# Layer norm of a 256 x 1024 activation: the root's Newton steps on GpSimd, the mean taken off on VectorE meanwhile

## The reference

```
def layer_norm(x, g, b):
    xf = x.astype(jnp.float32)
    mu = jnp.mean(xf, -1, keepdims=True)
    var = jnp.mean(jnp.square(xf - mu), -1, keepdims=True)
    y = (xf - mu) * lax.rsqrt(var + LN_EPS)
    return (y * g.astype(jnp.float32) + b.astype(jnp.float32)).astype(x.dtype)
...
x = layer_norm(alpha * x + mix, ln_g[l, 1], ln_b[l, 1])
```

## Time and profile before

| what | us |
|---|---|
| median of 3 runs (1609.17 to 1610.27) | 1610.07 |
| the profiled execution, whole | 1608.99 |
| its span in the profile | 1607.2 |
| PE busy | 1572.9 (98%) |
| DVE busy | 997.8 (62%) |
| ACT busy | 704.6 (44%) |
| POOL busy | 18.5 (1%) |

### The profile page before, as it was taken

One profiled execution on the slowest core, in us unless ns is written; L12 is line 12 of the kernel. 1 busy time (PEld: TensorE's weight loads), 2 busy tenths in 40 slices (PEclk: granted clock), 3 DMA queues, 4 the chain that ended last, 5 costly groups with the idle time before them and its releaser, 6 DMA issues.

```text
span 1607.2 us, 23932 instructions
## 1 busy us (share of the span) xinstructions
PE 1572.9 (98%) x10298; PEld 1425.8 (89%) x10298; DVE 997.8 (62%) x1282; ACT 704.6 (44%) x794; POOL 18.5 (1%) x77
## 2 busy tenths in 40 slices
PE   6999999999999999999999999999999999999997
PEld 6879998799899988999988899998999898789996
DVE  6776556768765567535677654466354768964546
ACT  4725344457354443334354343344343365343431
POOL 1000000000000000000000000000000000000000
PEclk9999999999999999999999999999999999999999
DMA  8346555543565556555463655546555563375551
GB/s 264 130 157 210 184 185 182 209 158 111 172 207 193 184 184 199 193 185 184 145 223 132 210 184 184 186 155 236 184 184 184 157 208 97 126 236 184 186 189 46
DMA packets 198456, 286.18 MB, mean 178 GB/s; under 512 B 9287, under 2 KB 167055, under 8 KB 198351
## 3 DMA queue, kind: packets, MB, share of 16 engines
q1 hardware_dynamic: 194943, 272.20, 51.5%
q0 software_dynamic: 3264, 11.93, 2.3%
q10 hardware_dynamic: 144, 0.52, 0.1%
HBM read 283.58 MB, written 1.05 MB: 177 GB/s over the span
## 4 chain that ended last, share of the span: by engine, by line
PE 84%; DVE 11%; ACT 3%; DMA 1%; issue 1%; SPq 0%; DVEq 0%; ACTq 0%
PE ps L395 79%; DVE wlo L293 2%; PE ps L428 2%; ACT whi L288 1%; DVE x L508 1%; DVE res L505 1%; DVE xt L467 1%; DVE stats L482 1%; DMA raw<-in_mla_w_dq 1%; DVE res L479 1%; DMA raw<-in_w_in_mlstm 1%; DVE nt L497 1%; PE ps L1509 1%; PE ps L1821 0%; PE ps L1314 0%
## 5 line engine op out<-in xcount | busy, mean ns | idle before, releaser
L395 PE MATMUL ps<-xt,whi 128*128 128x256 f32 x4016 | 727.8, 283 | 0.0
L293 DVE TENSOR_TENSOR wlo<-raw,whi 128x2048 fp32r<-128x2048 f32 (+2 forms) x259 | 576.0, 2254 | 116.0 <-ACT whi L288 115.5
L395 PEld LDWEIGHTS ps<-xt,whi 128*128 128x128 f32 x4016 | 629.7, 192 | 8.0 <-issue 3.6
L395 PE MATMUL ps<-xt,wlo 128*128 128x256 f32 x2008 | 568.2, 283 | 0.0
L288 ACT ACTIVATE whi<-raw 128x2048 fp32r<-128x2048 f32 (+2 forms) x262 | 483.5, 1879 | 20.2 <-DMA raw<-in_w_out 4.5
L395 PE MATMUL ps<-whi,yt 128*128 128x512 f32 (+1 forms) x1472 | 461.4, 386 | 1.7 <-DVE wlo L293 0.9
L395 PEld LDWEIGHTS ps<-xt,wlo 128*128 128x128 f32 x2008 | 385.2, 192 | 0.0
L395 PEld LDWEIGHTS ps<-whi,yt 128*128 128x128 f32 x1472 | 274.8, 188 | 56.9 <-DVE wlo L293 2.2
L395 PE MATMUL ps<-wlo,yt 128*128 128x512 f32 (+1 forms) x736 | 283.8, 386 | 0.0
L709 DVE SCALAR_TENSOR_TENSOR arena<-arena,ps 128x512 f32<-128x512 f32 x76 | 52.2, 686 | 368.9 <-issue 289.9
L395 PE MATMUL ps<-whi,xt 128*128 128x512 f32 (+4 forms) x778 | 220.0, 361 | 3.8 <-DVE wlo L293 2.8
(11 more groups left out here) (220 smaller groups left out, 710.9 us busy)
## 6 DMA issues: line engine op xcount, KB each, us to landing
raw<-in_ffn_w_up SPq DMA_DIRECT2D x76, 1024.0 KB, 5.3
raw<-in_ffn_w_down SPq DMA_DIRECT2D x76, 1024.0 KB, 4.9
raw<-in_ffn_w_gate SPq DMA_DIRECT2D x44, 1024.0 KB, 5.3
raw<-in_diff_w_qkv SPq DMA_DIRECT2D x12, 1024.0 KB, 5.2
raw<-in_w_in_conv SPq DMA_DIRECT2D x10, 1024.0 KB, 6.0
raw<-in_w_out SPq DMA_DIRECT2D x8, 1024.0 KB, 4.9
raw<-in_w_in_mlstm SPq DMA_DIRECT2D x7, 1024.0 KB, 7.5
raw<-in_w_in_mlstm SPq DMA_DIRECT2D x8, 768.0 KB, 4.2
```

Source lines behind the costliest of these rows:

```text
L293: nc.vector.tensor_tensor(wlo[:, u.slot, 0:u.size], raw[:, u.slot, 0:u.size], whi[:, u.slot, 0:u.size].bitcast(F32), ALU.subtract).then_in ...
L395: m = nc.tensor.matmul(out_, p, q, start=first and n == 0, stop=last and n == 2, skip_group_check=True)
```

## The change

After the seed, the six Newton instructions of each row block are issued by GpSimd instead of VectorE, as tensor_scalar with y (and w) as per-partition scalars, each waiting for the one before it. A new semaphore ln_seed tells GpSimd that v, w and the seed are there, and ln_root tells VectorE that the root is. VectorE issues both halves' (res - mean) * g right after the seed, without waits between them, then waits for ln_root and issues both halves' second instruction. v is now waited for before w is issued, and the seed is issued after w without a wait of its own. GpSimd's loop now runs over ten norms instead of nine, and the load of the next g and b follows its Newton steps.

```
-            link.mark(nc.vector.tensor_scalar_add(v, mv[:, t, 1:2], LN_EPS))
+            link(nc.vector.tensor_scalar_add(v, mv[:, t, 1:2], LN_EPS))
             link.mark(nc.vector.tensor_scalar(w, mv[:, t, 1:2], LN_EPS, -0.5, ALU.add, ALU.mult))
-            dve.wait_ge(link.s, link.n - 1)
-            link(nc.vector.tensor_scalar(y.bitcast(I32), v.bitcast(I32), -0.5, RSQRT_SEED,
-                                         ALU.mult, ALU.add))
-            for _ in range(3):
-                link(nc.vector.scalar_tensor_tensor(out=k, in0=y, scalar=w, in1=y, op0=ALU.mult,
-                                                    op1=ALU.mult))
-                link(nc.vector.scalar_tensor_tensor(out=y, in0=k, scalar=1.5, in1=y,
-                                                    op0=ALU.add, op1=ALU.mult))
+            nc.vector.tensor_scalar(y.bitcast(I32), v.bitcast(I32), -0.5, RSQRT_SEED,
+                                    ALU.mult, ALU.add).then_inc(ln_seed, 1)
             if t == 0:
                 dve.wait_ge(gb_loaded, 32 * (n + 1))
             for h in range(2):
                 half = slice(h * 512, h * 512 + 512)
-                link(nc.vector.scalar_tensor_tensor(
+                link.mark(nc.vector.scalar_tensor_tensor(
                     out=res[:, t, half], in0=res[:, t, half], scalar=mv[:, t, 0:1],
                     in1=gb[:, 0, half], op0=ALU.subtract, op1=ALU.mult))
+            dve.wait_ge(ln_root, 2 * n + t + 1)
+            for h in range(2):
+                half = slice(h * 512, h * 512 + 512)
+                dve.wait_ge(link.s, link.n - 1 + h)
                 nc.vector.scalar_tensor_tensor(
                     out=x[:, t, half], in0=res[:, t, half], scalar=y, in1=gb[:, 1, half],
                     op0=ALU.mult, op1=ALU.add).then_inc(ln_x, 1)
...
+        def ln_gpsimd(pool, step, n):
+
+            for t in range(TT):
+                w, k, y = nt[:, 1, TT + t:TT + t + 1], nt[:, 0, t:t + 1], rs[:, t:t + 1]
+                pool.wait_ge(ln_seed, 2 * n + t + 1)
+                for i in range(3):
+                    step(nc.gpsimd.tensor_scalar(k, y, w, y, ALU.mult, ALU.mult))
+                    if i < 2:
+                        step(nc.gpsimd.tensor_scalar(y, k, 1.5, y, ALU.add, ALU.mult))
+                    else:
+                        nc.gpsimd.tensor_scalar(y, k, 1.5, y, ALU.add, ALU.mult).then_inc(ln_root, 1)
+            if n < N_LN - 1:
+                pool.wait_ge(ln_x, 4 * (n + 1))
+                load_gb(pool, n + 1)
...
-            for n in range(N_LN - 1):
-                ln_gpsimd(pool, n)
+            step = Chain(pool, pool_step)
+            for n in range(N_LN):
+                ln_gpsimd(pool, step, n)
```

More of the change, by code:

```diff
@@ L345, in build @@
         acc_bank = sem("acc_bank")
+        ln_seed = sem("ln_seed")
+        ln_root = sem("ln_root")
+        pool_step = sem("pool_step")
         ln_x = sem("ln_x")
@@ L510, in ln_normal @@
                     op0=ALU.mult, op1=ALU.add).then_inc(ln_x, 1)
-        def ln_gpsimd(pool, n):
-            pool.wait_ge(ln_x, 4 * (n + 1))
-            load_gb(pool, n + 1)
+        def ln_gpsimd(pool, step, n):
[11 more added lines that the diff above has]
+                load_gb(pool, n + 1)
         def load_gb(pool, n):
```

## The result

The changed kernel takes 1628.49 us (median of 4 runs, 1625.97 to 1629.15), the kernel before 1610.17 beside it: a ratio of 1.0113, interval 1.01 to 1.0126. It is 18.3 us slower. The profiled execution is the shortest of the four, 1625.97 with a span of 1624.1, 16.9 longer than before's 1607.2.

A forecast was written before the change was run, and what follows sets the result against it. PE was taken to bound the kernel, busy 98% of the span, with VectorE counting only where PE waits. Delays of 10.35+0.37+0.74+0.44 = 11.9 us on the median 1610.07 gave 1622.0; range 1611 to 1637.

The forecast's parts named there:

- held back: Rival: GpSimd's first Newton instruction waits for VectorE's two subtractions, R 1.07 later, +26.9 us, 1637; chance 0.30.
- the prediction's own signs: Prediction wrong if the step is not near 0.52, the first instruction waits, or PE's restart follows half 1.
- PE waits for half 0: At row block 1, PE's restart comes 2.88 us after half 0's second instruction starts; half 1's catching up buys nothing.
- The hand-over to GpSimd: From the seed's end on VectorE to GpSimd's first Newton instruction: 0.31 us, taken from a GpSimd load.
- Six steps of 0.28 and five waits of 0.24: GpSimd's Newton chain in each row block: 2.88 us, against 1.34 on VectorE.
- Unheld: Main case: GpSimd's Newton steps run beside VectorE's subtractions without waiting, steps of 0.4 to 0.6, 1622 us; chance 0.50.
- The sum per norm: Row block 1 of norms 0 to 8: PE's restart 1.15 us later each, 10.35 together.
- R: Start of half 0's second instruction on VectorE: forecast S+3.47 instead of S+2.32, or S+4.54 if held.
- S: Start of the seed instruction in the kernel before, 109.83 in norm 0, row block 1; other times count from it.
- Row blocks 0: Delay where VectorE has no slack: 0.37 us each in norms 4 and 6, 0.22 each in 7 and 8.
- The delay given back: Rival: a late weight transfer, as after norm 7, swallows no more than 1 to 2 us; no separate chance given.
- Norm 9: No PE work follows; its last half, which opens the last output transfer, comes 0.37 us later.

The follow-up runs named there:

- Three kernels that keep their clock there: Against the changed kernel: subtraction input from PSUM, 1610.82 us; two Newton steps, 1614.34. Against the kernel before: both subtractions ahead of both second instructions, 1612.59.
- the second trace of the changed kernel: The changed kernel run again unaltered, as a control for later runs: 1627.09 us, ratio 1.0108 against the kernel before.
- root first: Against the changed kernel, VectorE waits for the root before it issues both halves' subtractions: 1633.94 us, ratio 1.0152 against the kernel before.
- VectorE's order: Against the kernel before, Newton stays on VectorE and both subtractions go ahead of both second instructions: 1612.59 us, ratio 1.0021.

## Why the prediction came out as it did

The forecast was 1622.0, slower; measured 1628.5, within the range and with the right sign. Its mechanism was not the one that acted: the rival "held back" was, at a smaller size than the 1637 forecast for it. By the prediction's own signs it failed: a step is 0.40 from start to start (111.74 to 112.55 is 0.81 for two), not 0.52, and the first instruction waits.

- **PE waits for half 0, and its restart follows at 2.88** behind half 0's second instruction. Right: in the changed kernel 113.65 to 116.53 is 2.88. The reordering on VectorE alone showed that half 1's catching up buys nothing.
- **The hand-over to GpSimd, 0.31.** It was 0.10. The load that I took it from is another kind of instruction. Back again it was 0.04 (113.35+0.26 to 113.65), forecast 0.06.
- **Six steps of 0.28 and five waits of 0.24, 2.88.** The instructions take 0.34 and 0.26, near the upper bound I had chosen (mean 0.30). The wait is not 0.24 but 0.10. Together 2.3 without a hold. This term was mis-sized by 0.6: one wait of GpSimd, between a memset and a select, does not price the wait between two steps.
- **Unheld.** This is the step that failed. GpSimd's first instruction was held by the two subtractions: it ran from 110.28 to 111.64, 1.36 instead of 0.34. With an input from PSUM it was not held, with one subtraction for 0.43. I had 1.07 for it in the rival; it is 1.02. The rule of the Trainium skill that I cited ("SBUF — State Buffer", "Who interferes with whom") is what this case then showed, and I had given it 0.30.
- **The sum per norm.** R was put at S+3.47 without the hold and S+4.54 with it. S is agg+0.43 in the kernel before (109.83-109.40). Counted from agg, so that it doesn't matter that this whole norm lies 0.14 later in the second trace, R is agg+4.11, that is S+3.68. The error of 0.8 in hand-over and waits and the missing hold of 1.02 nearly cancel, which is why 1.15 a norm was forecast and 1.34 to 1.40 came. A near hit in the sum was two misses in its terms.
- **Row blocks 0.** I counted norms 4, 6, 7 and 8, 1.2 in all. Norms 1 and 3 cost 0.34 each as well, and all six come to 2.5. Norms 1 and 3 have the same 0.15 of idle time behind row block 0 as norms 7 and 8, and I had called them free without looking at it.
- **The clock.** Not in the sum at all. A wait of PE of 2.3 to 2.4 was followed by some microseconds at 1.2 GHz after norm 7 in both traces of the changed kernel and after norm 1 in one of them; the growth there was 1.2 to 1.4 above that of the other norms (2.70 and 2.55 after norm 7, 2.75 after norm 1, others 1.34 to 1.42). After norm 7 the low clock took more than this difference shows, since 0.9 is given back there: an estimate is 2.70-1.37+0.9 = 2.2 for the 6.8 us at half clock, beside 1.4 for the 3.4 us after norm 1.
- **The delay given back.** I allowed 1 to 2 us for it, behind norm 7, and named a weight transfer as the place. Three kernels that keep their clock there give back 0.9; 0.72 of it is PE's wait for VectorE's small instruction (line 2103), not a transfer. In the changed kernel that wait is gone too, and the low clock covers it.
- **What is missing from the sum.** The first trace lies 16.9 above before's, 5.0 more than the 11.9 forecast: nine restarts 0.22 too small (2.0), row blocks 0 (1.3), the clock less what norm 7 gives back (1.3), the end (0.25), 4.85 together, and 0.15 that lay before the first norm. The median lies 1.4 further off than the profiled execution; no trace shows that part, though the second trace of the changed kernel, of an execution of 1627.30, has 1.4 more than the first behind norm 1, by the clock.
- **Norm 9.** Forecast 0.37 for its end, measured 0.62; the same error of R makes 0.21 of the difference.

Left open: the last 0.2 of what is given back behind norm 7; why the clock fell after a PE wait of 2.44 in one execution and not after 2.43 in another; and where it fell in the executions that were not profiled.

## What to carry to other kernels

Before work is moved to GpSimd to run beside VectorE, look at VectorE's inputs: an instruction with two SBUF inputs stopped a GpSimd instruction that reads SBUF until it was done here, and the overlap that was the point of the move was worth little: of the 1.34 that the two subtractions take, 1.02 came back as GpSimd's hold. With one input in PSUM the overlap was whole, and the kernel was as fast as before, not faster. Even then a chain of six dependent 128x1 instructions took GpSimd 2.3 us against VectorE's 1.34. To hide something in the gaps of such a chain, put independent instructions of the same engine into them, first the ones on which the first consumer waits.

## What the runs showed of the hardware that was not expected

- GpSimd's wait between two dependent small instructions is 0.10 us and its start behind VectorE's semaphore 0.10; its 128x1 tensor_scalar takes 0.34 with two per-partition scalars and 0.26 with one. The 0.24 that stood before a select is not general.
- The hold ends 0.14 to 0.22 after the end of VectorE's last instruction with two SBUF inputs, and the second of two that are issued back to back comes ahead of a GpSimd instruction that has already begun to wait: GpSimd was not let in between.
- Waits of PE that differ by 0.01 us (2.43, 2.44) were followed by the full clock in one execution and by half of it in another; waits of 1.02 and 0.80 close together were followed by half clock for 3.4 us, and in one execution (root first) a wait of 2.75 kept the full clock and one of 1.91 did not.
- A wait of PE can hide elsewhere: behind norm 7 with VectorE's order a restart that came 0.54 later did not make the next norm later, since a wait of 0.72 for VectorE's small instruction, 25 us on, was gone.
